# All adaLN weights issued from GpSimd's queue, with semaphores of their own, in a diffusion backbone of differential attention and a mixture of experts

## What is computed

```python
for i in range(2):
    sh1, sc1, ga1, sh2, sc2, ga2 = split(silu(c) @ w_ada[i] + b_ada[i])      # and the same from c_ctx
    h = rmsnorm(x) * (1 + sc1) + sh1                                         # both token groups
    q, k, v, f = split(h @ w_in[i])
    o = (softmax(q1 k1) - lam * softmax(q2 k2)) @ v                          # differential attention
    gates = sigmoid(h @ w_gate[i] + b_gate[i])
    out = (gates_a * (rmsnorm(o) @ w_attn_out[i]) + gates_f * (fourier(f) @ w_four_out[i])) @ w_out[i]
    x = x + ga1 * out
    h2 = rmsnorm(x) * (1 + sc2) + sh2
    x = x + ga2 * moe(h2)                # 16 experts, top 2 inside the best group of 4
```

## Time and profile before

| | before |
|---|---|
| median of three runs | 1579.85 us |
| the profiled execution | 1580.55 us, of it 1578.7 us span |
| PE busy | 1403.4 us (89%) |
| DVE busy | 789.6 us (50%) |
| ACT busy | 672.9 us (43%) |
| POOL busy | 98.4 us (6%) |
| DMA | 359.35 MB, mean 228 GB/s |
| mean granted TensorE clock | 0.938 of full |

### The profile page before, as it was taken

One profiled execution on the slowest core, in us unless ns is written; L12 is line 12 of the kernel. 1 busy time (PEld: TensorE's weight loads), 2 busy tenths in 40 slices (PEclk: granted clock), 3 DMA queues, 4 the chain that ended last, 5 costly groups with the idle time before them and its releaser, 6 DMA issues.

```text
span 1578.7 us, 20838 instructions
## 1 busy us (share of the span) xinstructions
PE 1403.4 (89%) x7774; PEld 1023.9 (65%) x7774; DVE 789.6 (50%) x1268; ACT 672.9 (43%) x1098; POOL 98.4 (6%) x98
## 2 busy tenths in 40 slices
PE   5799899997998996899999964999999887998882
PEld 2577677885556874788888853998875774543330
DVE  1512235423775626899999957465349643000002
ACT  4432113333665315588888853542357540111001
POOL 2100000000000000011121111000000000101001
PEclk8799999998998997799999986999999997999996
DMA  8752564335872231799999964363240358999994
GB/s 285 276 187 94 187 235 125 94 94 175 266 258 75 89 111 70 257 382 384 385 375 371 376 234 145 120 218 116 94 147 1 137 188 310 413 415 416 414 414 170
DMA packets 129365, 359.35 MB, mean 228 GB/s; under 512 B 14569, under 2 KB 14890, under 8 KB 128642
## 3 DMA queue, kind: packets, MB, share of 16 engines
q1 hardware_dynamic: 117522, 323.20, 56.3%
q0 software_dynamic: 10896, 31.87, 5.4%
q10 hardware_dynamic: 864, 3.15, 0.5%
HBM read 345.57 MB, written 25.17 MB: 235 GB/s over the span
## 4 chain that ended last, share of the span: by engine, by line
PE 74%; DMA 14%; DVE 5%; ACT 3%; issue 2%; POOL 0%; SPq 0%; POOLq 0%; ACTq 0%; DVEq 0%
PE ps L544 18%; PE ps L546 18%; PE ps L545 18%; DMA ring<-in_w_e_gate 9%; PE ps L796 3%; PE ps L1084 3%; PE ps L887 3%; PE ps L910 2%; PE ps L814 2%; PE ps L1106 1%; DMA ring<-in_w_e_down 1%; PE ps L898 1%; DMA w_raw<-in_w_in 1%; DMA w_raw<-in_w_ada 1%; PE ps L1027 1%
## 5 line engine op out<-in xcount | busy, mean ns | idle before, releaser
L540 DVE TENSOR_TENSOR w_lo<-w_raw,w_hi 128x1024 fp32r<-128x1024 f32 x224 | 270.7, 1223 | 342.2 <-ACT w_hi L536 340.0
L536 ACT ACTIVATE w_hi<-w_raw 128x1024 fp32r<-128x1024 f32 x224 | 235.7, 1059 | 360.4 <-PE ps L546 268.6
L544 PE MATMUL ps<-h_hi,w_hi 128*128 128x512 f32 (+1 forms) x704 | 250.6, 356 | 16.6 <-DVE h_lo L1526 9.1
L545 PE MATMUL ps<-h_lo,w_hi 128*128 128x512 f32 (+1 forms) x704 | 248.1, 352 | 0.0
L546 PE MATMUL ps<-h_hi,w_lo 128*128 128x512 f32 (+1 forms) x704 | 248.1, 352 | 0.0
L544 PEld LDWEIGHTS ps<-h_hi,w_hi 128*128 128x128 f32 x704 | 134.9, 192 | 39.3 <-DVE h_lo L1526 9.9
L546 PEld LDWEIGHTS ps<-h_hi,w_lo 128*128 128x128 f32 x704 | 134.8, 191 | 18.8
L545 PEld LDWEIGHTS ps<-h_lo,w_hi 128*128 128x128 f32 x704 | 134.8, 191 | 18.6 <-issue 0.2
L1084 PE MATMUL ps<-ring,xT 128*64 128x256 f32 x1024 | 131.0, 392 | 17.2 <-DMA ring<-in_w_e_up 9.8
L1084 PEld LDWEIGHTS ps<-ring,xT 128*64 128x64 f32 x1024 | 68.9, 138 | 80.1 <-DMA ring<-in_w_e_up 24.4
L540 DVE TENSOR_TENSOR w_lo_more<-w_raw,w_hi_more 128x1024 fp32r<-128x1024 f32 x96 | 115.3, 1222 | 5.2
(11 more groups left out here) (257 smaller groups left out, 2318.9 us busy)
## 6 DMA issues: line engine op xcount, KB each, us to landing
w_raw<-in_w_ada SPq DMA_DIRECT2D x96, 512.0 KB, 4.9
w_raw<-in_w_e_gate SPq DMA_DIRECT2D x64, 512.0 KB, 5.3
w_raw<-in_w_e_up SPq DMA_DIRECT2D x64, 512.0 KB, 7.4
w_raw<-in_w_e_down SPq DMA_DIRECT2D x64, 512.0 KB, 6.4
ring<-in_w_e_gate SPq DMA_DIRECT2D x64, 512.0 KB, 15.5
ring<-in_w_e_up SPq DMA_DIRECT2D x64, 512.0 KB, 15.4
ring<-in_w_e_down SPq DMA_DIRECT2D x64, 512.0 KB, 15.5
w_raw<-in_w_in SPq DMA_DIRECT2D x56, 512.0 KB, 4.3
```

Source lines behind the costliest of these rows:

```text
L536: act.activation(whi(n), raw[:, slot(n), :, :], ACT.Copy).then_inc(hi_ready, 1)
L540: dve.tensor_tensor(wlo(n), raw[:, slot(n), :, :], whi(n).bitcast(F32), ALU.subtract).then_inc(lo_ready, 1)
L544: pe.matmul(acc, sh, mh, start=first, stop=False, skip_group_check=True)
L545: pe.matmul(acc, sh, ml, start=False, stop=False, skip_group_check=True)
```

## The change

`ada_in`, four semaphores, takes the place of `raw_in[4..7]` for the adaLN chunks. All calls of `load_ada` leave SyncE's program and stand in GpSimd's: groups 0 to 4 at its start, with the vectors and small constants behind group 0; groups 5 to 11 behind the stores of zeros; groups 12 to 23 behind the save of `X` and ahead of its restore. The condition each transfer waits for is the same as before. The computing engines' programs are the same but for the semaphore's name.

```diff
+    ada_in = [sem(f"ada_in{k}") for k in range(AB)]
...
-        before = exp0[0] // WS if slot(n) < WS else 2 * AG * 4 // AB
+        before = exp0[0] // WS if slot(n) < WS else 0
...
-            sp.dma_start(raw[:, WS + m % AB, :, :], w_chunk(w_ada[layer], CK * ch, CW * g)).then_inc(raw_in[WS + m % AB], 16)
+            sp.dma_start(raw[:, WS + m % AB, :, :], w_chunk(w_ada[layer], CK * ch, CW * g)).then_inc(ada_in[m % AB], 16)
...
@@ SyncE
-        for b in range(4):
-            load_ada(sp, b)
         sp.dma_start(cst[:, C_TRI:], consts[:, C_TRI:]).then_inc(cst2_in, 16)
-        load_ada(sp, 4)
-        ada_loads = {n + WS - 1: b + 1 for n, b in ADA_AT.items() if b + 1 < AG}
...
                 load(sp, mix0[i] + n, chunk_of(i, s, ch))
-                if i == 0 and n in ada_loads:
-                    load_ada(sp, ada_loads[n])
-                if i == 0 and (s, ch) == (("WA", 1), 3):
-                    for b in range(AG, 2 * AG):
-                        load_ada(sp, b)
@@ GpSimd
-        load_vectors(pool, 1)
-        pool.dma_start(lamv[:, :, :], ...)
-        pool.dma_start(wr[:, :, :], ...)
-        pool.dma_start(brb[:, :], ...)
+        for b in range(5):
+            load_ada(pool, b)
+            if b == 0:
+                load_vectors(pool, 1)
+                (lamv, wr, brb as before)
         pool.wait_ge(filled, 3)
         pool.wait_ge(n_lo, KT)
         (eight stores to hsort)
...
+            if i == 0:
+                for b in range(5, AG):
+                    load_ada(pool, b)
             wait_all_emptied(pool, (i, "n1"))
             pool.wait_ge(roped[i], 1)
             pool.dma_start(xkeep, ...).then_inc(x_kept[i], 16)
+            if i == 0:
+                for b in range(AG, 2 * AG):
+                    load_ada(pool, b)
             pool.wait_ge(x_kept[i], 16)
@@ TensorE
-            pe.wait_ge(raw_in[WS + m_ % AB], 16 * (m_ // AB + 1))
+            pe.wait_ge(ada_in[m_ % AB], 16 * (m_ // AB + 1))
```

More of the change, by code:

```diff
@@ L667, in _ @@
         pool.memset(zrow[:, :], 0.0).then_inc(filled, 1)
-        load_vectors(pool, 1)
[L669 to L672, removed]
+        for b in range(5):
+            load_ada(pool, b)
+            if b == 0:
+                load_vectors(pool, 1)
+                pool.dma_start(lamv[:, :, :], lam_qk.rearrange("(a l) m d -> a (l m) d", a=1)
+                               .to_broadcast([P, 4 * DEPTH, HD])).then_inc(lam_in, 16)
+                pool.dma_start(wr[:, :, :], w_router.rearrange("(k p) n -> p k n", p=P)).then_inc(small_in, 16)
+                pool.dma_start(brb[:, :], b_router.rearrange("(a n) -> a n", a=1).to_broadcast([P, NE])).then_inc(small_in, 16)
         pool.wait_ge(filled, 3)
```

## The result

The change takes 1565.37 us, the median of four runs (1563.73 to 1566.36), against 1581.10 before (four runs, 1578.14 to 1583.06). The ratio is 0.9903 with a 95% interval of 0.9886 to 0.9920, so it is faster by 15 us (13 to 18). The forecast was 1565, range 1557 to 1575. The profiled execution took 1565.73 us, 1563.8 of it span.

What follows compares the result with a forecast made beforehand. The prediction took PE to set the pace (74% of the span), with time to be had only where it stands still: 1578.7 - 8.7 - 3.4 - 8.6 + 6 = 1564.0 us span, median 1565, range 1557 to 1575.

Steps and rivals of the forecast that it cites:

- A: Mixers, 166 to 178 us: PE's 5.79 us stop for a g_four bank and the slow clock behind it go; gain 8.7 us.
- B: Mixers, 213 to 219 us: PE's 1.81 us idle behind late stream chunks and the slow clock go; gain 3.4 us.
- D: Attention's start: PE's 7.29 us wait for adaLN chunk 48 goes, as layer 1's chunks load early; gain 8.6 us.
- The 0.8 us of clock: Attention's third score product: it ran at the lower clock; if the clock holds, another 0.8 us is gained.
- The start: Kernel's start, up to the sixteenth adaLN chunk: a loss of 6 us, between 0 and 17.
- Term (1): Start: POOL's adaLN loads beside the tokens delay them; 0 to 5.1 us, taken as 2.
- Term (2): Start, chunks 8 to 15: two rounds of slower issue and landing from POOL; 0 to 6.8 us, taken as 1.
- Term (3): Start: SP issues four GF chunks that share the DMA engines with adaLN chunks 12 to 15; 0 to 5.1, taken as 3.
- R1: Start is free or better, tokens landing in time and GF's chunks yielding: 1556 to 1561 us, chance 13%.
- R2: Start is dear, its terms at their upper halves, 12 to 17 us: time 1570 to 1577 us, chance 13%.
- R3: Mixers: A and B come back through ACT's and DVE's order, only D is won: 1577 us, chance 9%.
- R4: Attention held by POOL's loads: landing L costs (L - 7.9) x 12 us, whole gain gone from 9.2; slower 8%, mild 5%.

Runs made afterwards that it cites:

- e2: Kernel before, with only adaLN groups 5 to 11 (chunks 20 to 47) moved to GpSimd's queue: ratio 0.9925 to before, 11.9 us faster.
- e4: Kernel before, all adaLN loads kept on SyncE, groups 5 to 11 four stream loads later, group 12 right behind them: 1564.16 us, ratio 0.9883 to before.
- e1: Kernel before, with only layer 1's adaLN chunks (48 to 95) moved to GpSimd's queue: ratio 0.9939 to before, 9.6 us faster.
- e3: The edits of e1 and e2 together: groups 0 to 4 by SyncE as before, 5 to 23 by GpSimd; 1561.50 us, ratio 0.9872 to before.
- e10: e3, with GpSimd waiting for the tokens to land before issuing its vectors and small constants: 1558.26 us, ratio 0.9863 to before.
- e5: The change, with SyncE holding the first GF chunk until PE has used the sixteenth adaLN chunk: 1561.83 us, ratio 0.9877 to before.
- e9: The change with the edits of e5 and e6 together: 1562.40 us, ratio 0.9883 to before.
- e11: The change, with three adaLN chunks in flight in attention in place of four: 1577.36 us, ratio 0.9975 to before.
- e6: The change, with GpSimd waiting for the tokens to land before its first adaLN chunk, vectors and small constants: 1563.44 us, ratio 0.9893 to before.
- e8: The change, with two adaLN chunks in flight in attention in place of four: 1598.12 us, ratio 1.0104 to before.

## Why the prediction was right

**Stream chunks out of the line (A and B), 12.1 us forecast.** 13.1 by the landmarks of the change and of e2, 11.9 by e2's ratio. The mechanism is shown by e2 and, from the other side, by e4: it is the order that counts, not the queue. That the banks would then be emptied in time was put at nothing and came out so: no wait for a bank stands in their place. As the prediction said of its signs, ACT waits for PE and not for DMA in the mixers, and the clock is 1.00 from 80 us to attention; between 60 and 80 us it is 0.92, F having begun 5 us later.

**Layer 1's chunks early (D), 8.6 forecast.** 7.7 by the landmarks, 7.9 by those of e1, 9.6 by e1's ratio. The next thing in PE's way was the first item's exponentials, as said. The 0.8 us of clock was there (1.13 us in place of 1.97 for the third score product), but PE gave as much back at 377.21, in a wait of 0.91 us for chunk 53, issued only on use. e1, e3 and e10 have the same wait (0.69 to 0.78 us), and so has e4 (0.86 and 0.29), where SyncE issues, so it is not POOL's doing. That term was counted to its full, and should have stood near nothing.

**The start, 6 us of loss forecast.** 5.0 by the landmarks, 4.9 by e3's ratio. Term (1), the tokens: 2 forecast, 1.4 measured. Term (2), POOL's slower issue and landing: 1 forecast; e5 and e9, with POOL, take 12.4 and 12.7 from the 8th to the 16th chunk, the six with SyncE 12.0 to 13.1, so no such loss is seen. Term (3), GF's loads beside the last chunks: 3 forecast, 3.5 by e5's median and 3.8 by the table's means (16.3 less 12.5). That GF's loads delay the last chunks is shown by e5; that they do it by taking a share of the DMA engines' rate is argued, for the rates don't say it plainly: 274 GB/s in the change against 326 in e5 from 41 to 46 us, and 397 against 312 from 46 to 52. So the sum was right within 1 us, with term (2) not seen and term (3) about as measured.

**The total.** That it met the measured median within 0.4 us is in part luck: by the landmarks the three parts were off by 1.0, 0.9 and 1.0 us, and of the two gains one came out larger and one smaller.

**Nothing for the rest.** Groups 5 to 11, the save and the restore of `X` and the zeros moved behind adaLN loads in POOL's queue at no cost: PE's list of waits has none that leads there.

**The rivals.** R1 and R2 (start free or dear) are out by the landmarks. R3 is out by e2. R4, attention held by its loads, did not come: chunks landed in 5.0 us there. But its price was read from a formula that e11 showed too kind: three chunks in flight already cost 8 us of attention where the formula had room to spare. It counts the use of a chunk as room, so with four in flight too the waits would begin about 0.6 us below the 7.9 us given (an estimate), and the 9.2 lies as much too high. With four in flight it was not measured.

The Trainium skill (SBUF — State Buffer, "SBUF: two separate sides") says that VectorE can lock GpSimd out and so hold up the descriptors of its DMAs, while VectorE runs an operation in a two-port mode. No such hold-up is seen here: POOL's issues in attention took 0.70 to 0.72 us each beside a VectorE that was busy 74.1 of 100 us, and landings were 5.0 us. Whether any of VectorE's operations there was of that kind no run here shows, so this doesn't speak against the page; the prediction left the condition out. What the Trainium skill says of spreading DMAs over queues (DMA: Bandwidth & Descriptors, "Rules for kernel authors") agrees with e4: against a better order in one queue, the second queue gave at most the 2.7 us between e3 and e4, whose intervals overlap.

## What to carry to other kernels

A queue whose transfers wait for different consumers is a line: ask of each waiting transfer what stands behind it and how long the wait lasts, and then either give it a queue of its own or put it where its condition is already met; here both gave nearly the same. A queue that is freed also issues sooner what nobody needs yet, and that can slow what is on the critical chain: hold the eager loads back by a wait, or leave the urgent part as it was (e5, e3). The gain of a removed wait is bounded by the next thing in the way, which can be read from the same rows, and a room worked out from the mean rate of use overstates the slack (e11).

## What was not expected of the hardware

POOL's queue moved the same bytes in fewer packets: 129,365 before and 117,078 after, 12,287 fewer. By queue, SyncE's (q1) went from 117,522 packets to 91,410 and POOL's (q0) from 10,896 to 24,720 for the same 50.3 MB, which is 272 and 144 for each of the 96 loads; one packet more elsewhere makes up the difference. The 128 between them is one for each partition, so it seems that two rows of 2 KB went as one packet of 4 KB. It didn't make the transfers faster: 5.0 us to landing in attention against 4.6. Before, then after:

```profile
DMA packets 129365, 359.35 MB, mean 228 GB/s; under 512 B 14569, under 2 KB 14890, under 8 KB 128642
```

```profile
w_raw<-in_w_ada SPq DMA_DIRECT2D x48, 512.0 KB, 4.6
```

```profile
DMA packets 117078, 359.35 MB, mean 230 GB/s; under 512 B 14570, under 2 KB 14891, under 8 KB 116355
```

An issue from POOL's queue took 0.72 us (96 in 68.8 us), from SyncE's mostly 0.37.

The granted clock in the first 25 us is not the same even between kernels that are alike up to there. In the window from 16 to 24 us it was 0.79 to 0.88 in e6, e8, e10 and e11, where the stretch from the tokens to the first adaLN chunk is 11.1 to 11.2 us, and 0.60 to 0.76 in the others, where it is 12.2 to 13.0. That is as large as some of the effects measured here, so terms of one or two microseconds in the start were read from intervals that begin behind it.
